# A seventh place in the ring of expert weights, the last w_down quarters in pieces, empty places left out of gathers and scatters, and two loads no longer held for the first gather

## What is computed

```python
lg = (hf @ w_rg).astype(jnp.float32) + b_rg          # 4 groups
g_top = jnp.argmax(lg, axis=-1)                      # one group for each token
top_v, top_i = lax.top_k(le_g, TOP_K_INNER)          # 2 of the 4 experts in it
a = jnp.einsum('nd,edf->nef', hf, w_gate)
b = jnp.einsum('nd,edf->nef', hf, w_up)
hid = jax.nn.silu(a) * b * gates[..., None].astype(a.dtype)
y = jnp.einsum('nef,efd->nd', hid, w_down)
```

## Time and profile before

| | us |
|---|---|
| median of 3 runs (1054.82 to 1057.53) | 1055.14 |
| the profiled execution | 1056.41 |
| its span, from the first to the last instruction | 1054.6 |
| TensorE busy | 952.0 (90%) |
| DMA, mean over the span | 326 GB/s |

### The profile page before, as it was taken

The page is one execution under the profiler, slowest core; times in us unless marked ns, Lnnn a source line. Parts: engine busy times, 40 slices in busy tenths (PEclk is TensorE's granted clock), DMA queues, the critical chain, the costliest instruction groups (busy, mean ns, idle before and its releaser), DMA issues.

```text
span 1054.6 us, 10922 instructions
## 1 busy us (share of the span) xinstructions
PE 952.0 (90%) x4761; PEld 558.8 (53%) x4761; DVE 265.5 (25%) x378; ACT 142.0 (13%) x325; POOL 47.2 (4%) x86
## 2 busy tenths in 40 slices
PE   4999999999989999999959999978899789987875
PEld 4777777777766667777745334322343224422331
DVE  2005989791243430110142101100011101101101
ACT  5111112121124440000010110001000010000100
POOL 3000010102010000000000000000000000000000
PEclk9999999999999999999979999989999899998988
DMA  9954699963958987528459799999999999999991
GB/s 318 371 209 170 216 404 400 370 226 133 342 205 330 347 327 263 181 95 327 182 222 362 309 372 422 422 423 421 422 421 423 421 422 421 422 423 421 422 411 51
DMA packets 80101, 343.96 MB, mean 326 GB/s; under 512 B 6765, under 2 KB 10711, under 8 KB 54151
## 3 DMA queue, kind: packets, MB, share of 16 engines
q1 hardware_dynamic: 60175, 296.45, 70.6%
q10 hardware_dynamic: 15808, 33.84, 8.7%
q0 software_dynamic: 4064, 12.91, 3.3%
HBM read 330.76 MB, written 12.24 MB: 325 GB/s over the span
## 4 chain that ended last, share of the span: by engine, by line
PE 72%; DMA 23%; DVE 1%; ACT 1%; issue 1%; SPq 0%; POOL 0%; ACTq 0%; POOLq 0%; DVEq 0%
PE PS L844 69%; DMA ring<-in_w_up 12%; DMA ring<-in_w_down 7%; DMA ring<-in_w_gate 2%; DMA small<-in_small 1%; PE PS L873 1%; PE PS L859 1%; PE PS L909 1%; DMA x_scr<-Z 1%; DMA X<-x_scr,pidx 1%; PE PS L1107 1%; DVE Z L1688 0%; SPq L464 0%; DVE HT L1688 0%; POOL out_y L560 0%
## 5 line engine op out<-in xcount | busy, mean ns | idle before, releaser
L844 PE MATMUL PS<-HT,ring 128*128 128x288 f32 x1536 | 382.9, 408 | 0.7 <-issue 0.6
L844 PEld LDWEIGHTS PS<-HT,ring 128*128 128x128 f32 x1536 | 288.1, 190 | 86.7 <-issue 9.5
L844 PE MATMUL PS<-ring,Z 128*64 128x512 f32 (+2 forms) x1056 | 246.3, 602 | 34.2 <-DMA ring<-in_w_up 17.2
L844 PEld LDWEIGHTS PS<-ring,Z 128*64 128x64 f32 (+2 forms) x1056 | 88.4, 144 | 179.2 <-issue 175.6
L844 PE MATMUL PS<-ring,HT 128*64 128x512 f32 x480 | 120.7, 630 | 11.0 <-DMA ring<-in_w_up 7.2
L844 PEld LDWEIGHTS PS<-ring,HT 128*64 128x64 f32 x480 | 39.2, 145 | 81.8 <-issue 81.6
L844 PE MATMUL PS<-Z,X 128*128 128x256 f32 x128 | 41.7, 459 | 10.7 <-DMA X<-x_scr,pidx 5.0
L844 PEld LDWEIGHTS PS<-Z,X 128*128 128x128 f32 x128 | 32.9, 325 | 27.3 <-issue 13.0
L1748 DVE TENSOR_TENSOR Z<-Z,PS 128x512 f32<-128x512 f32 x8 | 5.5, 688 | 157.8 <-PE PS L844 157.8
L670 ACT ACTIVATE aux<-PS 128x288 f32<-128x288 f32 x32 | 13.2, 411 | 227.0 <-PE PS L844 227.0
L1688 DVE TENSOR_TENSOR Z<-PS,ln2R 128x512 f32<-128x512 f32 x16 | 11.1, 691 | 122.4 <-PE PS L844 122.4
(11 more groups left out here) (211 smaller groups left out, 547.5 us busy)
## 6 DMA issues: line engine op xcount, KB each, us to landing
ring<-in_w_gate SPq DMA_DIRECT2D x31, 2048.0 KB, 17.9
ring<-in_w_down SPq DMA_DIRECT2D x31, 2048.0 KB, 20.1
ring<-in_w_up SPq DMA_DIRECT2D x29, 2048.0 KB, 16.0
ring<-in_w_in ACTq DMA_DIRECT2D x12, 2048.0 KB, 16.0
ring<-in_w_o SPq DMA_DIRECT2D x8, 2048.0 KB, 13.4
ring<-in_cache_v SPq DMA_DIRECT2D x8, 1536.0 KB, 7.7
ring<-in_cache_v SPq DMA_DIRECT2D x32, 384.0 KB, 8.9
ring<-in_cache_k SPq DMA_DIRECT2D x24, 384.0 KB, 7.7
```

What stands on the lines that cost most here:

```text
L844: return pe.matmul(out, lhsT, rhs, start=start, stop=stop, skip_group_check=True)
```

## The change

- **Seventh place.** The ring has seven places, (4, 5, 6, 0, 1, 2, 3), with `aux` as number 6, for all 96 loads; places 7 and 8 are used once, for loads 7 and 8. Load i waits, each by itself, for the quarter that held load i − 7 (i − 9 for loads 9 to 15).
- **Hold.** Load 7 no longer waits for the first gather; the waits for the stores and the squares stay.
- **Pieces.** In the last pair both quarters of w_down come in four pieces of 1 MB as the second w_up quarter did. `down` starts on the first two, goes through its first 128 rows of hidden units for all four column blocks, and then waits for the others.
- **Empty places.** All gathers and scatters have a bound on the index, and a row whose number is above it is left out. Gathers 3 and 4 now read the list of targets, in which empty places are out of bounds; gathers 1 and 2 read the old list with number 0. The fifth gather is issued only in the branch that needs it, and nothing waits for it at the end.

```diff
+    RING = (4, 5, 6, 0, 1, 2, 3)
+    def ring_slot(i):
+        if i < 9:
+            return (RING + (7, 8))[i], 1
+        return RING[(i - 9) % 7], 2 + (i - 9) // 7
...
                 for j in range(12):
...
+                    i = 48 * it + 12 * k + j if isinstance(it, int) else None
...
+                    elif i == 7:
+                        sp.wait_ge(x1_stored, 16 * 8)
+                        sp.wait_ge(x1_last, 32)
+                        sp.wait_ge(squares, 3 + 15)
+                    elif i >= 9:
+                        both = 1 if last and k == 3 and j in (6, 8, 10) else 0
+                        before = i + both - (9 if i < 16 else 7)
+                        done, ahead = QUARTERS[before // 2 % 6]
+                        sp.wait_ge(done, before // 12 + 1 + ahead)
-                    if last and k == 3 and j in (6, 7):
+                    if last and k == 3 and j >= 6:
                         for e in range(2):
-                            load(k, 6 + e, j - 5)
+                            load(k, j // 2 * 2 + e, 1 + j % 2)
...
             pool.indirect_dma_start(
                 out=XG[n], out_offset=None, in_=x1_scr,
                 in_offset=bass.IndirectOffsetOnAxis(ap=pidx[:, at:at + 1], axis=0),
+                bounds_check=TOK - 1, oob_is_err=False,
             ).then_inc(gathered[n], 16)
...
-                stage_rows(it * 2 + (n + 2), 0, n, it * 4 + (2 * n + 4))
+                stage_rows(it * 2 + (n + 2), 1, n, it * 4 + (2 * n + 4), 53)
                 pool.wait_ge(scattered[n], it * 16 + 16)
                 pool.sem_inc(pool_turn, 1)
-                if not (last and n):
+                if not last:
                     gather(n)
...
-                for n, count in at:
-                    pe.wait_ge(landed[n], count)
+                split = last and k == 3
+                if split:
+                    pe.wait_ge(piece_in[1 + half], 32)
+                else:
+                    for n, count in at:
+                        pe.wait_ge(landed[n], count)
                 w = [slots[n].rearrange("p (f n) -> p f n", n=D) for n, _ in at]
                 for g in range(8):
-                    f, q = (g % 2, g // 2) if half else (g // 4, g % 4)
+                    f, q = (g % 2, g // 2) if half and not split else (g // 4, g % 4)
+                    if split and g == 4:
+                        for n, count in at:
+                            pe.wait_ge(landed[n], count)
```

More of the change, by code:

```diff
@@ L300, in build @@
     gathered = [sem(f"gathered{n}") for n in range(2)]
-    part_done, part_added, piece_in, half_out = (sem(n) for n in ("part_done", "part_added", "piece_in", "half_out"))
+    part_done, part_added, half_out = (sem(n) for n in ("part_done", "part_added", "half_out"))
+    piece_in = [sem(f"piece_in{n}") for n in range(3)]
     scattered = [sem(f"scattered{n}") for n in range(2)]
@@ L351, in build, with slot_of @@
     slots = [ring[:, n, :] for n in range(SLOTS)] + [aux[:, :], Z[:, 4096:8192], Z[:, 8192:12288]]
-    FIRST_SLOTS = (4, 5, 6, 0, 1, 2, 3, 7, 8, 4, 5, 0)
+    RING = (4, 5, 6, 0, 1, 2, 3)
     LATER_SLOTS = (1, 2, 3, 4, 5, 0, 1, 2, 3, 4, 5, 0)
+    def ring_slot(i):
+        if i < 9:
+            return (RING + (7, 8))[i], 1
+        return RING[(i - 9) % 7], 2 + (i - 9) // 7
+    LOADS = [sum(ring_slot(i)[0] == n for i in range(12 * NE // 2)) for n in range(SLOTS)]
+    BASE_LATER = [BASE_MOE[n] + LOADS[n] - (15 if n in (1, 2, 3) else 16) for n in range(SLOTS)]
     QUARTERS = ((g0_used, 0), (gate_done, 0), (u0_used, 0), (up_done, 1), (d0_used, 1), (down_done, 1))
[L356 to L360, removed]
+    def slot_of(it, k, j):
+        if isinstance(it, int):
+            n, nth = ring_slot(48 * it + 12 * k + j)
+            return n, 16 * (BASE_MOE[n] + nth)
         n = LATER_SLOTS[j]
-        return n, it * 128 + 16 * (BASE_MOE[n] + 2 * k + (j + 3) // 6)
+        return n, it * 128 + 16 * (BASE_LATER[n] + 2 * k + (j + 3) // 6)
     @block.sync
@@ L446, in _, with experts @@
         sp.wait_ge(s_added, 2 * PAIRS)
-        def experts(it, par8, first=False, last=False):
+        def experts(it, par8):
+            last = isinstance(it, int) and it == 1
             def load(k, j, pieces=0):
@@ L453, in load @@
                 name = ("w_gate", "w_up", "w_down")[q // 2]
-                n, _ = slot_of(first, it, k, j)
+                n, _ = slot_of(it, k, j)
                 w = a[name][0, bass.ds(par8 * 8 + 2 * k + e, 1)]
@@ L467, in load @@
                     sp.dma_start(dst[:, r:r + 1, :], src[:, half * 2 + r:half * 2 + r + 1, :]
-                                 ).then_inc(landed[n] if r else piece_in, 16)
+                                 ).then_inc(landed[n] if r else piece_in[q - 3], 16)
             def quarter_done(k, q):
@@ L476, in experts @@
                 for j in range(12):
[L477 to L496, removed]
@@ L498, in experts @@
+                    if last and k == 3 and j >= 6:
                         for e in range(2):
-                            load(k, 6 + e, j - 5)
+                            load(k, j // 2 * 2 + e, 1 + j % 2)
                     else:
                         load(k, j)
-        experts(0, 0, first=True)
-        experts(1, 1, last=True)
+        experts(0, 0)
+        experts(1, 1)
         sp.wait_ge(idx_ready, 1)
@@ L561, in scatter_columns @@
                                            in_=XG[1][:, half * D // 2:(half + 1) * D // 2], in_offset=None,
-                                           element_offset=half * D // 2)
+                                           element_offset=half * D // 2, bounds_check=2 * TOK - 1, oob_is_err=False)
         def scatter(n, added):
@@ L616, in _ @@
             pool.sem_inc(pool_turn, 1)
+            gather(0)
             gather(1)
@@ L1195, in up @@
             def up(k, bank, w_half, done):
-                at = [slot_of(first, it, k, 4 * bank + 2 * w_half + e) for e in range(2)]
+                at = [slot_of(it, k, 4 * bank + 2 * w_half + e) for e in range(2)]
                 split = last and k == 3 and bank and w_half
                 if split:
-                    pe.wait_ge(piece_in, 32)
+                    pe.wait_ge(piece_in[0], 32)
                 else:
@@ L1226, in down @@
                         pe.wait_ge(out_moved, it * 16 + 4 * k)
-                at = [slot_of(first, it, k, 8 + 2 * half + e) for e in range(2)]
-                for n, count in at:
-                    pe.wait_ge(landed[n], count)
+                at = [slot_of(it, k, 8 + 2 * half + e) for e in range(2)]
+                split = last and k == 3
[4 more added lines that the diff above has]
+                        pe.wait_ge(landed[n], count)
                 w = [slots[n].rearrange("p (f n) -> p f n", n=D) for n, _ in at]
                 for g in range(8):
-                    f, q = (g % 2, g // 2) if half else (g // 4, g % 4)
+                    f, q = (g % 2, g // 2) if half and not split else (g // 4, g % 4)
+                    if split and g == 4:
+                        for n, count in at:
+                            pe.wait_ge(landed[n], count)
                     ff = half * 2 + f
@@ L1525, in _ @@
         did(dve.memset(R, 0.0))
-        did(dve.memset(pidx[:, NQ:NQ + 2], 0))
+        did(dve.memset(pidx[:, 2 * NQ + 2:2 * NQ + 4], TOK))
         did(dve.memset(GT, 0.0))
```

23 lines of the change are left out of this document (17 added, 6 removed).

## The result

| | before | after |
|---|---|---|
| median of five runs, us | 1055.14 (1053.98 to 1057.53) | 1047.75 (1044.96 to 1050.56) |
| ratio to before, 95% interval | 1 | 0.9929 (0.9908 to 0.995) |
| the profiled execution, us | 1056.41 | 1047.75 |
| its span, us | 1054.6 | 1045.9 |
| packets and MB of the software queue (gathers and scatters among them) | 4064, 12.91 | 3920, 9.25 |

What follows compares the result with a forecast made beforehand. Bound by a queue of bytes at 421 GB/s from 616 us, before that paced by TensorE and the first gather. Terms sum to −12.4 us, against the median 1055.14: 1042.7 us forecast, range 1038.5 to 1049.5.

Steps and rivals of the forecast that it cites:

- hold taken off: First gather, now beside loads 7 and 8, takes 10.0 us instead of 5.9, delaying releases up to 616 us: +4.1 us.
- seventh place: Load 12 fills the idle queue at 586 to 592 us, putting it one load ahead: −5.0 us.
- fifth gather: Dropping this 1.05 MB transfer from the middle of the full stretch: −2.5 us.
- empty places, in the stretch: Scatters and gathers in the full stretch leave out 247 rows, 2.02 MB: −4.8 us.
- empty places, last scatter: On the path at the end, the last scatter's second half leaves out 71 of 128 rows: −0.7 us.
- last quarters in pieces: Behind the last w_down landing 16 matmuls remain instead of 32: −3.5 us.
- A: Scatters and gathers: empty places cost as before, since skipped rows might still be moved; 1048.2 us, chance 0.13.
- B: First gather lands behind both loads 7 and 8, after 14.5 us instead of 10.0; 1047.2 us, chance 0.12.
- C: At the end, TensorE's clock falls in the pieces, cancelling their gain; 1046.2 us, chance 0.09.
- F: Two or three of A to C together: −3.2 to +1.1 us, 1052 to 1056 us, chance 0.07.
- rule of turns: DMA engines alternate between queue rows with work, so the first gather beside loads gets half the rate: +2.5 us.
- Rival D: Gathers and scatters: checking indices against the bound is dear, at 6 us each +5.6 us, 1060.7 us; chance 0.06.

Runs made afterwards that it cites:

- e1: Changed kernel with the wait on the first gather ahead of load 7 put back; 1042.96 us, ratio 0.9868.
- e7: Kernel before the change with only load 7's wait on the first gather taken out; 1061.66 us, ratio 1.0046.
- e5: Changed kernel with a ring of six places instead of seven; 1053.66 us, ratio 0.9965.
- e9: Changed kernel with the fifth gather, all 128 rows, and the wait for it at the end put back; 1052.05 us, ratio 0.9953.
- e6: Changed kernel with every place moved, empty ones too, the bounds still looked at; 1051.0 us, ratio 0.9953.
- e4: Changed kernel with the last pair's w_down quarters as whole loads again; 1051.69 us, ratio 0.9955.
- e3: Changed kernel with load 7's wait on the first gather put back and each group's places dealt out evenly over the partitions; 1038.92 us, ratio 0.9839.

## Why the prediction was right or wrong

| term | forecast | measured | from |
|---|---|---|---|
| hold taken off | +4.1 | +6.1 | after and before; 5.9 by e1, 5.7 by e7 |
| seventh place | −5.0 | −4.8 | e5 |
| fifth gather | −2.5 | −2.2 | e9 |
| empty places, in the stretch | −4.8 | −1.2 | e6; −0.7 against after alone |
| empty places, last scatter | −0.7 | −0.4 | e6, within the noise of the tail |
| last quarters in pieces | −3.5 | −3.5 | e4 |
| sum | −12.4 | −6.0 | |

−6.0 lies in the measured interval, −5.3 to −9.7 us, and near the 5.7 by which the two profiles differ without the path and the time ahead of the gather.

1047.75 lies in the range because the range took in the times of rivals A and B. The sum itself missed by two terms, both too favourable, by 2.0 and 3.6 us. That the time fell between A's and B's while neither came true as put is luck. (By the prediction's own prices B and C together would be −4.4 and A and C −3.4, so F reached further down than its −3.2.)

- **What bounds the kernel** held: a queue of bytes from 624 on, paced by TensorE before, and by the first gather before that.
- **The hold**: the mechanism was right, the size was not. I took the second gather's 10.0 as "the same pair of loads". The late start is the same, 4.2 and 4.4 us, but the first gather's last count comes 2 us later, and why stays open. Load 5 was no part of it, as it had landed before the issue, against what rival B says. The gather did not land with load 8 (4.9 us ahead of it), so B as put is wrong, but nearly half of its price came true. By the rule of turns alone (+2.5) I would have been further off.
- **The empty places** are the step that failed. Two sentences of it were wrong. "A row left out is a packet left out": the pair of a scatter and a gather still has 288 packets after, with 0.80 MB instead of 2.10 for groups 1 and 3, and the packets under 512 B rose from 112 to 280 in the same 30 us. These are the DMA rows of after for 795 to 825 (packets and bytes of all queues; below, the software queue's packets, MB and share of the engines):

```profile
DMA packets 1822, 12.64 MB, mean 421 GB/s; under 512 B 280, under 2 KB 280, under 8 KB 280
...
q0 software_dynamic: 288, 0.80, 6.6%
```

  They cost little, though: that share of 6.6% is 0.39 of before's 16.8%, and the bytes are 0.38. What cost the forecast 3.6 us is the other: dividing bytes by 421 GB/s gives the mean of sixteen engines, and a landing waits for the last of them. In the mean of the sixteen counts 3.3 to 4.6 us did come out. Rival A's time, 1048.2, and B's, 1047.2, are both as near to 1047.75 as the noise can tell, but A's reason, that the empties are moved, is false.
- **Seventh place, fifth gather, pieces** came out within 0.3 us, the seventh place where it was said (586 to 592 filled, later breaks still there).
- **Rival C** did not happen. In the last two bursts of after the clock was granted in full, behind waits of 1.2 and 1.4 us: 16 matmuls in some 3.6 us each. **Rival D** is out: e1's gather, with the bound looked at, takes 6.15, and e3's 5.93. At the very end POOL's second half scatter is issued 1.60 us behind the first instead of 1.29, which takes part of the last scatter's gain.
- **First wait for a load**: 701, not 721. The landing that ends it comes 0.6 us later behind the first gather's issue than in before, where the prediction had the queue 2.2 us earlier by then (0.9, and 1.3 for 65 rows).

## What to carry to other kernels

A hold is worth its place when what it holds has nowhere to go next: ask for the load behind it, not for the load. A small transfer on the critical path is worth an empty queue; a single large one beside it cost 5.5 us. Bytes taken out of a queue that several engines share are worth what the engine that ends last saves; here, spread evenly over partitions, they counted about in full (3.9 and 5.4 us for 4.8).

## What the runs showed of the hardware

- A gather of 1 MB took 5.9 to 6.2 us with no load issued beside it (before, e1, e3). Where one or two loads of 2 MB were issued 0.1 to 1.0 us ahead, it took 10.0 to 12.6. Its first packet then comes 4.2 to 4.9 us after the issue instead of 1.7 to 1.9; then it gets about half of the engines' time (48.9% in after).
- A row that an indirect transfer leaves out because of its index leaves a packet of under 512 B, and next to no time (288 packets as before, 0.80 MB instead of 2.10, 6.6% of the engines' time instead of 16.8%).
- Rows left out unevenly did not show in the DMA share before the end: it stayed at 1.01 until 1016, and only then took 9 us to run down instead of 4. They showed earlier in the sixteen counts of each load (1.8 us apart in e1 ahead of the first such transfer, 8.9 behind the second). With the same bytes left out evenly the counts of the last load lay 3.3 to 4.4 us apart.
